# Router matrix, bias and norm columns of the second kind of routing stage: buffers of their own, loaded in the mixer ahead

## The reference, cut to what matters

```python
for i in range(DEPTH_2):                      # 2 layers
    mix = _retention_diff_mixer(...) if i % 2 == 0 else _mla_gla_mixer(...)
    x = _layer_norm(ALPHA * x + mix, ln1_g[i], ln1_b[i])
    ffn = _hier_moe(x, moe_w_grp[i], moe_b_grp[i], moe_w_exp[i], moe_b_exp[i], ...)
    x = _layer_norm(ALPHA * x + ffn, ln2_g[i], ln2_b[i])

def _hier_moe(x, w_grp, b_grp, w_exp, b_exp, w_gate, w_up, w_down):
    grp_logits = (xf @ w_grp + b_grp)                     # 512 tokens x 4
    g_idx = argmax(grp_logits); p_grp = softmax(grp_logits)[g_idx]
    exp_logits = (xf @ w_exp + b_exp).reshape(n, 4, 8)    # 512 x 32
    top_l, top_e = top_k(exp_logits of the group, 2)
    gate = p_grp * softmax(top_l)
    ...                                                   # experts on the chosen tokens, summed
```

## Time and profile before

| | us |
|---|---|
| median of 3 runs | 2740.08 |
| lowest, highest | 2737.75, 2744.41 |
| the profiled execution | 2749.82 |
| its span | 2748.0 |
| TensorE busy | 2522.1 |
| VectorE busy | 913.8 |
| ScalarE busy | 646.9 |

### The profile page before, as it was taken

How to read it: one execution, slowest core, us unless ns; L and a number is a source line. 1 busy time by engine, 2 the same in 40 slices (tenths; PEclk the granted TensorE clock), 3 DMA queues, 4 the chain that set the end, 5 groups by cost and what they waited for, 6 DMA issues and landing times. The chain is left out here.

```text
span 2748.0 us, 42579 instructions
## 1 busy us (share of the span) xinstructions
PE 2522.1 (92%) x17694; PEld 1273.5 (46%) x17694; DVE 913.8 (33%) x2037; ACT 646.9 (24%) x1329; POOL 259.8 (9%) x249
## 2 busy tenths in 40 slices
PE   7999898999999999999899998998998899999896
PEld 3554785443433334445444444443356544444442
DVE  2656353412211121567453110013525572210004
ACT  4423763310110010333221110112334221111101
POOL 0100363200000000000110000000004120000001
PEclk9999898999999999999999999999999999999999
DMA  9324305789999963001579999996004149999996
GB/s 322 109 74 161 103 7 199 303 365 427 428 429 428 428 276 133 24 0 62 188 303 406 427 428 428 427 417 214 0 1 191 51 184 371 427 426 427 428 427 262
DMA packets 117170, 735.83 MB, mean 268 GB/s; under 512 B 28695, under 2 KB 32051, under 8 KB 77440
## 3 DMA queue, kind: packets, MB, share of 16 engines
q1 hardware_dynamic: 105808, 703.12, 62.7%
q0 software_dynamic: 7488, 29.10, 2.7%
q10 hardware_dynamic: 3696, 1.06, 0.2%
HBM read 708.31 MB, written 32.55 MB: 270 GB/s over the span
## 5 line engine op out<-in xcount | busy, mean ns | idle before, releaser
L2650 PE MATMUL bank<-ring,expert_in 128*64 128x512 f32 (+1 forms) x1840 | 427.9, 593 | 17.8 <-DMA ring<-in_moe_w_up_dram 8.0
L2668 PE MATMUL bank<-ring,hidden_T 128*64 128x512 f32 (+1 forms) x896 | 226.9, 595 | 34.7 <-ACT hidden_T L2524 29.8
L2650 PEld LDWEIGHTS bank<-ring,expert_in 128*64 128x64 f32 (+1 forms) x1840 | 135.9, 128 | 237.4 <-issue 237.2
L2379 DVE TENSOR_TENSOR hidden<-silu_gate,bank 128x512 f32<-128x512 f32 x32 | 33.7, 1054 | 576.3 <-PE bank L2650 462.8
L2620 PE MATMUL bank<-onehot,x_part 128*128 128x128 bf16 x3072 | 178.0, 220 | 0.0
L2620 PEld LDWEIGHTS bank<-onehot,x_part 128*128 128x128 bf16 x3072 | 173.2, 98 | 2.4 <-issue 2.4
L1956 PE MATMUL bank<-ring,expert_in 128*64 128x512 f32 x768 | 169.7, 598 | 4.9 <-DMA ring<-in_w_gate_dram 4.9
L2668 PEld LDWEIGHTS bank<-ring,hidden_T 128*64 128x64 f32 (+1 forms) x896 | 67.1, 129 | 137.2 <-issue 101.8
L2508 ACT ACTIVATE expert_in<-bank 128x512 f32<-128x512 f32 x64 | 35.0, 595 | 400.3 <-PE bank L2620 400.3
L2650 PE MATMUL bank<-home,expert_in 128*64 128x512 f32 (+1 forms) x320 | 112.4, 593 | 8.0 <-DMA ring<-in_moe_w_up_dram 8.0
L3611 PE MATMUL bank<-x_cols,ring 128*128 128x512 f32 x256 | 112.5, 593 | 1.3 <-PEq L220 1.3
(11 more groups left out here) (718 smaller groups left out, 3932.3 us busy)
## 6 DMA issues: line engine op xcount, KB each, us to landing
ring<-in_moe_w_gate_dram SPq DMA_DIRECT2D x48, 2048.0 KB, 22.9
ring<-in_moe_w_down_dram SPq DMA_DIRECT2D x44, 2048.0 KB, 27.5
ring<-in_moe_w_up_dram SPq DMA_DIRECT2D x42, 2048.0 KB, 25.1
ring<-in_w_gate_dram SPq DMA_DIRECT2D x24, 2048.0 KB, 23.3
ring<-in_w_up_dram SPq DMA_DIRECT2D x24, 2048.0 KB, 21.1
ring<-in_w_down_dram SPq DMA_DIRECT2D x24, 2048.0 KB, 26.7
ring<-in_w_mod_dram SPq DMA_DIRECT2D x12, 2048.0 KB, 10.0
home<-in_moe_w_gate_dram SPq DMA_DIRECT2D x8, 2048.0 KB, 16.9
```

Source lines behind the costliest of these rows:

```text
L2650: mm = pe.matmul(B[2 + 2 * part][rows, :], xe[:, c, rows], ws[e](c), start=(c == 0), stop=(c == NC - 1))
L2668: mm = pe.matmul(B[6 + b][rows, :], hT[:, c, rows], ws[e](c)[:, b * COLS:(b + 1) * COLS], start=(c == 0), stop=(c == NF - 1))
```

## The change

The router's matrix, its bias and the norm's columns get buffers that live through the whole program, and a semaphore that lives as long. A new function, `load_router`, issues the six loads. It is called in `even_mixer` behind the distance table for layer 0, and in `gated_linear_attention` behind the expert loads for layer 1. `settle_second` issues them no longer, and `fold_router` waits for 96 in layer 0 and 192 in layer 1.

```diff
--- before.py
+++ after.py
@@ -139,12 +139,15 @@
         self.const = sb("const", [P, len(CONST_NAMES), P])
         self.const_dram = const
         self.eps = sb("eps", [P, 2])
+        self.router_w, self.router_b = sb("second_router_w", [P, NC, 36]), sb("second_router_b", [P, 36])
+        self.ln_cols = sb("second_ln_gain_and_shift_cols", [P, 2, NC])
         self.psum = [ctx.enter_context(nc.psum_tensor(f"bank{i}", [P, 512], F32)) for i in range(8)]
         self.weights_loaded = [sem(f"weights_loaded{i}") for i in range(RING)]
         self.weights_used = sem("weights_used")
         self.rows_here = [sem(f"rows_here{i}") for i in range(NT * CHOICES)]
         self.rows_cleared = sem("rows_cleared")
         self.rows_stored = sem("taken_rows_stored")
+        self.router_here = sem("second_router_loaded")
         self.z_parked = [sem(f"z_parked{t}") for t in range(NT)]
         self.mod_stored = sem("mod_stored")
         self.more_loaded = [sem(f"more_weights_loaded{i}") for i in range(MORE)]
@@ -230,6 +233,18 @@
 def columns(vec, p=P):
 
     return vec.rearrange("(c p) -> p c", p=p)
+
+
+def load_router(m, eng, I, i):
+
+    at = 0
+    for name in ("grp", "exp"):
+        k = I[f"moe_w_{name}_2"].shape[2]
+        eng.dma_start(m.router_w[:, :, at:at + k], I[f"moe_w_{name}_2"][i].rearrange("(c p) e -> p c e", p=P)).then_inc(m.router_here, 16)
+        eng.dma_start(m.router_b[:, at:at + k], I[f"moe_b_{name}_2"][i].partition_broadcast(P)).then_inc(m.router_here, 16)
+        at += k
+    for j, name in enumerate(("g", "b")):
+        eng.dma_start(m.ln_cols[:, j, :], columns(I[f"ln1_{name}_2"][i]), allow_slow_non_contiguous=True).then_inc(m.router_here, 16)
 
 
 def w_cols(w, a, b):
@@ -3169,8 +3184,7 @@
     small = [(m.const_dram[:, len(CONST_NAMES) + SEG_NAMES.index(n), :]) for n in ("slot_iota", "lt")]
     with stage(m) as (sem, sb):
         gain, shift = sb("ln_gain", [P, D]), sb("ln_shift", [P, D])
-        w, b = sb("router_w", [P, NC, NL]), sb("router_b", [P, NL])
-        ln_cols = sb("ln_gain_and_shift_cols", [P, 2, NC])
+        w, b, ln_cols = m.router_w, m.router_b, m.ln_cols
         shifted_w, w_sums = sb("router_w_by_shift", [P, NC, NL]), sb("router_w_sums", [P, 2, NL])
         lt, lt16, one16 = sb("lt", [P, P]), sb("lt16", [P, P], BF16), sb("one16", [P, P], BF16)
         xT = sb("x_cols", [P, NC, P])
@@ -3182,7 +3196,7 @@
         top, idx = sb("top", [P, NT, 8]), sb("top_index", [P, NT, 8], U32)
         lane0 = sb("expert_lane", [P, E])
         sel = sb("chosen_experts", [P, NT, E], BF16)
-        ln_here, router_here, tables_here = sem("ln_loaded", "router_loaded", "tables_loaded")
+        ln_here, tables_here = sem("ln_loaded", "tables_loaded")
         w_order, w_summed, w_spread, w_ready = sem("router_order", "router_w_summed", "router_w_spread", "router_w_ready")
         (evacuated, stat_order, stats_ready, rooted, ln_order, shifted) = sem(
             "evacuated", "stat_order", "ln_stats_ready", "ln_rooted", "ln_order", "rows_shifted")
@@ -3201,13 +3215,6 @@
                 sp.dma_start(gain[:, :], I["ln1_g_2"][i].partition_broadcast(P)).then_inc(ln_here, 16)
                 sp.dma_start(shift[:, :], I["ln1_b_2"][i].partition_broadcast(P)).then_inc(ln_here, 16)
                 sp.dma_start(early[0][0][:, :, :], early[0][1]).then_inc(m.more_loaded[0], 16)
-                at = 0
-                for name, k in (("grp", GR), ("exp", E)):
-                    sp.dma_start(w[:, :, at:at + k], I[f"moe_w_{name}_2"][i].rearrange("(c p) e -> p c e", p=P)).then_inc(router_here, 16)
-                    sp.dma_start(b[:, at:at + k], I[f"moe_b_{name}_2"][i].partition_broadcast(P)).then_inc(router_here, 16)
-                    at += k
-                for j, name in enumerate(("g", "b")):
-                    sp.dma_start(ln_cols[:, j, :], columns(I[f"ln1_{name}_2"][i]), allow_slow_non_contiguous=True).then_inc(router_here, 16)
                 sp.dma_start(R.lane[:, :], small[0]).then_inc(tables_here, 16)
                 sp.dma_start(lt[:, :], small[1]).then_inc(tables_here, 16)
                 m.load_until(sp, m.moe2[i] + RING)
@@ -3349,7 +3356,7 @@
                 wo = Order(dve, w_order)
 
                 def fold_router():
-                    dve.wait_ge(router_here, 96)
+                    dve.wait_ge(m.router_here, 96 * (i + 1))
                     for j, to in ((1, shifted_w), (0, w)):
                         by = ln_cols[:, j, :].unsqueeze(2).to_broadcast([P, NC, NL])
                         wo.then(dve.tensor_tensor(to[:, :, :], w[:, :, :], by, ALU.mult))
@@ -3593,6 +3600,7 @@
                 sp.dma_start(tabR, rot["retention"]).then_inc(turn_here, 16)
                 sp.wait_ge(m.weights_used, base + 12)
                 sp.dma_start(dt, dist).then_inc(far_here, 16)
+                load_router(m, sp, I, 0)
                 sp.wait_ge(turned, UNITS)
                 sp.wait_ge(weighed, UNITS)
                 sp.wait_ge(stat_ready, HEADS)
@@ -4060,6 +4068,7 @@
                 sp.dma_start(crosses[:, :, :], m.const_dram[:, at + first:at + first + LEVELS, :]).then_inc(tables_here, 16)
                 sp.dma_start(gain[:, :], columns(I["od_gla_norm_2"][0]), allow_slow_non_contiguous=True).then_inc(gain_here, 16)
                 m.load_until(sp, upto)
+                load_router(m, sp, I, 1)
                 sp.wait_ge(gain_here, 16)
 
             @block.tensor
```

## The result

| | before | changed |
|---|---|---|
| median of 6 runs, us | 2743.97 | 2728.07 |
| lowest, highest | 2737.75, 2752.54 | 2725.57, 2729.68 |
| the profiled execution | 2749.82 | 2725.57 |
| its span | 2748.0 | 2723.8 |

The ratio is 0.9937, 95% interval 0.9921 to 0.9953: faster by 0.6%, 15.9 us between the medians, and the interval leaves out 1. The prediction was 18.6 us less, a ratio of 0.9932.

What follows compares the result with a forecast made beforehand. TensorE, busy nearly throughout, was taken as the bound, with waits, low clock or loads as openings. Stage gains 10.9 + 7.7 = 18.6 us, so 2740.1 - 18.6 = 2721.5 us; range 2717 to 2730.

Steps and rivals of the forecast that it cites:

- The wait goes: TensorE's wait at the spread product for VectorE's fold disappears: 8.13 us saved in the first routing stage, 4.51 in the second.
- The clock comes back: Spread product to end of first logits runs at full clock: 3.7 us saved in the first routing stage, 3.2 in the second.
- The tables: First routing stage: `slot_lane` and `lt` land at 1324.8, so routing tile 0 starts at 1329.7, saving 10.9 us, not 11.8.
- Nothing late in the second stage: Second routing stage: tables land in time, twelve records (5.4 us) cover 4.3 us of routing, and 7.7 us passes on.
- 10.9 us in the first stage: First routing stage: tile 0's routing starts 10.9 us sooner and `count(0)` passes that on; bounds 6.6 and 11.8.
- rival A: First routing stage: a 3.6 us wait at `count(0)` drops the clock, losing 3.7 us; gain 14.9, 2725.2 us; chance 0.19.
- a clock below 1.00 after `count(0)`: Sign of being wrong: the clock was to be 1.00 through the first 20 us of each routing stage.
- The sum by the rows of this case: Both routing stages: 10.9 plus 7.7 gives 18.6 us, using this kernel's 9.8 us row for a small load behind 2 MB.
- The gain passes through the experts: Expert stretches: loads follow TensorE's slot releases, so the full gain counts and the stretches last as long as before.
- What is added costs nothing: Both mixers: six added loads, at most 35 us of SP's time, covered by waits of 124.8 and 75.6 us; cost 0.
- A mixer longer than before: Sign of being wrong: either mixer, where the six loads are added, takes longer than before.

Runs made afterwards that it cites:

- only-first-stage kernel: Against the kernel before, only layer 0's six loads moved to the mixer, layer 1's left in its routing stage: median 2738.02 against 2746.08, ratio 0.9964.
- the dose of 7.0 us: Changed kernel plus 8 idle TensorE products ahead of the projection in the second routing stage: median 2735.48 against the changed kernel's 2728.33.
- small loads first: Kernel before, with the six router loads issued ahead of everything else on SP in the routing stage: median 2739.62 against 2746.08, ratio 0.9967.

## Why the prediction was right, and where not

**The wait goes: right.** The fold starts 0.30 us after the stage's start and TensorE's spread product waits in neither stage. 8.13 and 4.51 us were the sizes in the trace of before, and they are what went.

**The clock comes back: right.** From the spread product to the end of the first logits I had 6.4 us for the changed kernel. It takes 6.19 in the first stage (1311.90 to 1318.09) and 6.18 in the second (2161.47 to 2167.65).

**The tables: right.** I placed them 11.6 us after the stage's start; `lt` is taken at 11.4 (1314.64), and they landed 9.4 and 9.6 us after their issue, behind the 2 MB load. With the tables in front the wait is gone.

**Nothing late in the second stage: nearly right.** 7.7 us forecast, 7.4 measured. Routing tile 0 was put at 4.3 us, under the 5.4 us of the twelve records; it took 5.5, and TensorE waited 0.47 us for it.

**10.9 us in the first stage: wrong, it is 7.4.** This is the step that failed, although the total came out near. Two terms were missing or mis-sized. First, routing tile 0 was put at 4.1 us, the duration it has in the trace of before; it took 5.5, because it now runs beside the whole of GpSimd's split of the same tile; without the split it took 3.0. In the kernel before, VectorE reached it when half of that split was over. The wait at `count(0)` was 4.97 us and not 3.6. Second, the clock fell within that wait, and the low clock behind it took 2.5 us. That was rival A, with 0.19; it came true, at a lower price than the 3.7 us I gave it. It also meets one of the signs I had set for being wrong, a clock below 1.00 after `count(0)`. Start to `count(0)` is 21.79 us where I had 20.7; the other 2.5 us are the clock. The sum by the rows of this case was 18.6; by rival A 14.9, and the stages gave 14.8. That these two agree so closely is luck: A had the clock 1.2 us too dear and no term for the slower routing, 1.1 us in the first stage and 0.3 in the second. That the forecast of the whole is only 2.7 us off has its share of luck too, since the medians differ by more than the stages.

Rival A was weighed by the length of the wait: I put 3.6 us between a 2.58 that left the clock alone and a 4.31 that did not. The two kernels with 2.5 to 2.6 us on either side, and the 3.17 us without a fall, show that this reading was unsound; that its direction came out is luck.

**The gain passes through the experts: right,** by the stretches of the only-first-stage kernel and by the dose of 7.0 us. TensorE's waits for the expert loads of both layers fell, from 30.6 and 29.5 us in the two profiles of before to 26.1.

**What is added costs nothing: right for the loads, with a bound too low.** SP in the second mixer of the changed kernel:

```profile
2072.61 1.07 SPq L185 DMA_DIRECT2D ring<-in_moe_w_up_dram  x2
2073.73 1.49 SPq L243 DMA_DIRECT2D second_router_w<-in_moe_w_grp_dram  x1
2075.26 22.37 SPq L244 DMA_DIRECT2D second_router_b<-in_moe_b_grp_dram  x1
2097.68 0.61 SPq L243 DMA_DIRECT2D second_router_w<-in_moe_w_exp_dram  x1
...
2101.82 0.58 SPq L247 DMA_DIRECT2D d_ln_gain_and_shift_cols<-in_ln_b_dram  x1
```

One load of 2 KB held SP for 22.37 us, behind 12 MB issued in the 11 us before, when I had bounded each issue by 5.88. SP was free at 2102.40, and the stage ends at 2149: 47 us of cover are left. In the first mixer the six issues are over in 6 us.

A mixer longer than before was another of my signs for being wrong, and the second mixer is: 269.7, 271.8 and 267.7 us in three profiles of the changed kernel, 267.8 and 268.0 in two of before. The six loads are not the cause. The kernel in which only the first stage's loads are moved has none of them in the second mixer, and took 271.8 us. What differs is how long the granted clock is low in it, added up over windows of 2 us: 20.5 us in both profiles of before, and 23.9, 27.3 and 20.5 us in the three of the changed kernel, in the order above; 27.3 in the one without the loads. The lengths follow these. Why the clock is low for longer in some executions is open.

**Open.** The medians differ by 15.9, 17.8 and 16.9 us in three comparisons, the stages by 14.8. In all ten comparisons of a kernel with the new buffers the medians differ by as much as the two routing stages or up to 5.5 us more; in the one with small loads first, which has the old buffers, they differ by 1.8 us less. The first mixer starts at 1046.1, 1047.9 and 1052.7 us in the three profiles of kernels with the old buffers, and between 1035.3 and 1045.9 in the eleven with the new. My expectation for the second profile of before was written so that 1046.1 fits both sides, so it settles nothing. Some us of the first block may go with where the buffers lie; no run separates that from scatter.

## What to carry to other kernels

When a wait goes, look for the next thing that the released engine needs, and also for what now runs at the same time as it: an instruction's duration read from a trace holds only beside the neighbours it had there. A small load takes its time from the queue it stands in, so ask what is in front of it, and don't move a group of small loads ahead of another without counting who is then last. Time the stages of a profile and not only the whole, when the whole scatters by more than the change.

## What the runs showed of the hardware

VectorE's small 128x32 addition took 0.19 us alone and 1.10 us beside GpSimd's 128x512 subtraction, and routing a tile 5.5 us instead of 3.0. The granted clock fell behind waits of 2.52 and 2.62 us in one kernel, and not behind 2.58 and 2.64 us in another or 3.17 us in a third. The issue of one 2 KB load held SP for 22.37 us with 12 MB issued ahead of it, and the same issue for 0.57 us at the head of a stage (small loads first).
